# Low halves of the second weight forms made by a negative copy on ScalarE and an adding DMA from GpSimd

## The chip, the cores and the metric

One core of one Trainium2 chip runs the whole program. The metric is the device time of one execution in microseconds. The core has TensorE (PE: matrix products, results in PSUM banks), VectorE (DVE), ScalarE (ACT), GpSimd (POOL), SyncE (SP, which here only issues loads) and 16 DMA engines.

## The reference, cut to what matters

Two layers on 512 tokens of width 1024, all in fp32. Each layer has two feed-forward blocks (FFNs) around an attention and a mixing part:

```python
def swiglu(x, wgu, wd):
    gate, up = jnp.split(x @ wgu, 2, axis=-1)
    return (jax.nn.silu(gate) * up) @ wd
...
h = h + 0.5 * swiglu(rms_norm(h, ffn1_norm[i]), ffn1_wgu[i], ffn1_wd[i])
```

The hidden width is 2816, that is 22 tiles of 128. The change touches only the four FFNs (F = 0 to 3).

## The kernel before, in words

Every fp32 operand is split into a rounded high half (ACT copies it into a tensor of type fp32r) and a low half, operand minus high half. A product is three matmuls: high by high, high by low, low by high.

In an FFN the first 4 hidden tiles are computed plainly. The other 18 (`FAST = 18`, numbered q) are "half-size products": the weights of a tile are four blocks a21, a22, a11, a12, loaded into `sraw[q % 2]` by two DMAs of 512 KB from SP. A fast matrix scheme with fewer block products, each on 256 token columns instead of 512, needs sums of these blocks. For each q there are

- `form_sums(q)` (DVE, three instructions, L1427, L1431, L1433): block sums into `sums`, of which there is only one copy. Its first instruction waits for `second_forms` of q-1;
- the first forms, `form_hi`/`form_lo`, 2048 wide: `first_plain` and `first_sums`, each a copy on ACT (L798, L804) and a subtraction on DVE (L1437, L1442);
- the second forms, `more_hi`/`more_lo`, two buffers of 1536: `second_plain(q)` (512 wide, from `sraw`; ACT L812, then DVE L1447) and `second_sums(q)` (1024 wide, from `sums`; ACT L816, then DVE L1452). The DVE halves of these two are what is replaced. The first raises `s_split`, which lets SP load tile q+2 into the same `sraw` buffer; the second raises `second_forms`, which lets PE start step 4 of q and DVE overwrite `sums`.

PE's order is written out by hand. In iteration n it does step 1 of tile n, step 4 of tile n-1, some down-projection products (`gap(n, 0)`), steps 2 and 3 of tile n, `gap(n, 1)`, steps 5 and 6 of tile n-1, and `gap(n, 2)`. A gap of the iterations from n = 4 on has 3, 3 and 2 such products; in iterations 1 to 3 it has 2, 1 and 1. Step 2 of q needs `first_sums(q)`; step 4 of q needs `second_forms` of q.

The orders on the other engines are fixed too. In iteration n >= 4 DVE does: product of tile n-2, `second_plain(n)`, low half of the hidden tile n-2, sums into h, `second_sums(n)`, `gate0(n)`, `first_plain(n+1)`, `up1(n-1)`, sums into h, `form_sums(n+1)`, perhaps a `down_split`, `first_sums(n+1)`, sums into h, perhaps a `down_split`, `gate1(n-1)` (L1401), and the rest of tile n-1. With r = (n-4) mod 3, two of the `down_split`s lie before `gate1` at r = 0, one at r = 2 and none at r = 1. In iterations 1 to 3 `gate1(n-1)` comes before `first_sums(n+1)`. ACT ends its iteration n with

```python
if n:
    fast_silu_(n - 1)
if n and n + 1 < FAST:
    second_plain(n + 1)
    second_sums(n + 1)
```

and `fast_silu_(n-1)` (L782) waits for `gate1(n-1)` (`x_read`). ACT's next work is `fast_hid(n-1)` (L787) and `copy_y(n+1)` (L825). GpSimd has no work inside the loop before: its first waiting instruction is the clearing of `sumsq` after the last `second_forms` of the FFN.

Of the kernel before, what the change touches and what calls it, by code (L numbers as in the profile page):

```python
# [108 lines left out]
def macaron_kernel(nc, x, mem, positions, ffn1_norm, ffn1_wgu, ffn1_wd, mix_norm, w_in,  # L109
# [12 lines left out]
    with ctx:  # L122
        def sem(name):
            return ctx.enter_context(nc.semaphore(name))
# [213 lines left out]
        wn_ready = sem("wn_ready")  # L338
        d_done = sem("d_done")
# [96 lines left out]
        def fast_no(F, q):  # L436
            return F * FAST + q + 1
# [51 lines left out]
        def _(sp):  # L489
# [25 lines left out]
            def ffn_loads(L, up, wgu, wd):  # L515
                F = 2 * L + (up == UP2)
                for kind, i in FFN_ORDER:
                    if kind == "S":
                        if i < 2:
                            sp.wait_ge(w_used, used(L, up + 1))  # L520
                        else:
                            sp.wait_ge(s_split, fast_no(F, i - 2))
                        col = fast_tile(i) * P
                        for a, c in ((1024, col), (0, col + FF)):
                            sp.dma_start(sraw[i % 2][:, a:a + 1024].rearrange("p (k c) -> p k c", c=P),
                                         wgu[L, :, c:c + P].rearrange("(k p) c -> p k c", p=P)).then_inc(s_loaded[i % 2], 16)
                        continue
# [49 lines left out]
        def _(pool):  # L577
# [36 lines left out]

            for L in range(0, LAYERS):
                inverse_rms(L * 4 + 1)
                stage_sums(L, 0, 1)
# [22 lines left out]
                inverse_rms(L * 4 + 4)  # L640
                stage_sums(L, 3, 4)
# [4 lines left out]
        def _(act):  # L646
# [99 lines left out]
            def ffn(L, f, up, stage, rb_no, gain, next_gain, next_unit):  # L746
# [60 lines left out]
                def second_plain(q):  # L807
                    if q < 2:
                        act.wait_ge(n_done, F + 1)
                    else:  # L810
                        act.wait_ge(second_product, step_no(F, q - 2, 3))
                    act.activation(more_hi[:, q % 2, 1024:1536], sraw[q % 2][:, 512:1024], ACT.Copy).then_inc(second_rounded, 1)  # L812

                def second_sums(q):
                    act.wait_ge(form_summed, 3 * fast_no(F, q))
                    act.activation(more_hi[:, q % 2, 0:1024], sums[:, 0:2, :].rearrange("p a c -> p (a c)"), ACT.Copy)\  # L816
                       .then_inc(second_rounded, 1)
# [379 lines left out]
        def _(dve):  # L1197
# [124 lines left out]
            def ffn(L, f, up, stage, stat_no, next_gain, next_unit):  # L1322
# [122 lines left out]
                def second_plain(q):  # L1445
                    dve.wait_ge(second_rounded, 2 * (fast_no(F, q) - 1) + 1)
                    dve.tensor_tensor(out=more_lo[:, q % 2, 1024:1536], in0=sraw[q % 2][:, 512:1024],  # L1447
                                      in1=more_hi[:, q % 2, 1024:1536].bitcast(f32), op=ALU.subtract).then_inc(s_split, 1)

                def second_sums(q):  # L1450
                    dve.wait_ge(second_rounded, 2 * fast_no(F, q))
                    dve.tensor_tensor(out=more_lo[:, q % 2, 0:1024], in0=sums[:, 0:2, :].rearrange("p a c -> p (a c)"),  # L1452
                                      in1=more_hi[:, q % 2, 0:1024].bitcast(f32), op=ALU.subtract).then_inc(second_forms, 1)

# [43 lines left out]
                if at_first:  # L1498
# [32 lines left out]
                    second_plain(0)  # L1531
# [4 lines left out]
                    second_sums(0)  # L1536
# [6 lines left out]
                else:  # L1543
# [28 lines left out]
                    second_plain(0)  # L1572
# [4 lines left out]
                    second_sums(0)  # L1577
# [10 lines left out]
                for n in range(FAST):  # L1588
# [3 lines left out]
                    if n >= 2:  # L1592
                        fast_product_(n - 2)
                        second_plain(n)
# [6 lines left out]
                    if n >= 4:  # L1601
                        second_sums(n)
                    gate0(n)
                    gate0_scale(n)
                    if n in (2, 3):
                        second_sums(n)
# [4 lines left out]
                    if n == 0:  # L1611
                        second_plain(1)
                        second_sums(1)
# [1054 lines left out]
```

## Time and profile before

| | |
|---|---|
| Time before | 2100.7 us, median of 2 runs (2100.58 to 2100.82) |
| Span of the profiled execution | 2098.5 us; its own time is not listed apart, and the runs lie 2.1 to 2.3 us above the span |
| PE | 2084.8 us busy, 99% of the span |
| VectorE | 1645.2 us, 78% |
| ScalarE | 986.8 us, 47% |
| GpSimd | 149.6 us, 7% |
| DMA | 212.14 MB, mean 101 GB/s |
| TensorE clock granted | 0.998 of full |

PE is the engine to watch: it is busy all through the span. The busy share of another engine says how full its queue is, not whether it delays anything.

### The profile page before, as it was taken

The page shows a single profiled execution, that of the slowest core. Times are in us where ns is not written, and L with a number is a line of the kernel's source. Part 1 is how long each engine was busy: PE and PEld are TensorE (multiplying, and loading weights), DVE is VectorE, ACT ScalarE, POOL GpSimd, SP SyncE. Part 2 cuts the span into 40 slices and gives each one's busy share as a digit, 9 for nine tenths or more (in the row PEclk, how much of TensorE's full clock was granted, in tenths as well). Part 3 has the DMA queues.
Part 4 walks back from the last instruction along what each step waited for, and adds up shares of the span by engine and source line. Part 5 has one row for each costly group of instructions (what it writes and reads, how often), then busy time and mean ns, then how long its engine had stood idle before and what let it go on. Part 6 is the DMA issues. An engine that isn't in the chain of part 4 may idle for free.

```text
span 2098.5 us, 32639 instructions
## 1 busy us (share of the span) xinstructions
PE 2084.8 (99%) x13143; PEld 1867.3 (89%) x13143; DVE 1645.2 (78%) x2460; ACT 986.8 (47%) x1491; POOL 149.6 (7%) x114
## 2 busy tenths in 40 slices
PE   9999999999999999999999999999999999999998
PEld 7999998889888889999889999988898888999997
DVE  7998886658654789888799988766686458898885
ACT  6444444446433544444454444343464345444442
POOL 0000003100120300000110000030002111000001
PEclk9999999999999999999999999999999999999999
DMA  6333323323231343332233333243233224333321
GB/s 197 101 112 99 103 86 113 124 81 101 96 106 41 92 129 107 118 100 91 75 116 116 106 111 106 66 142 99 81 102 104 77 66 135 91 111 103 100 85 56
DMA packets 268018, 212.14 MB, mean 101 GB/s; under 512 B 7422, under 2 KB 234332, under 8 KB 267868
## 3 DMA queue, kind: packets, MB, share of 16 engines
q1 hardware_dynamic: 264608, 205.55, 31.5%
q10 hardware_dynamic: 3260, 4.51, 0.8%
q8 instruction: 105, 1.72, 0.3%
q14 instruction: 45, 0.37, 0.1%
HBM read 207.93 MB, written 2.10 MB: 100 GB/s over the span
## 4 chain that ended last, share of the span: by engine, by line
PE 98%; ACT 1%; issue 0%; DVE 0%; POOL 0%; POOLq 0%; DVEq 0%; ACTq 0%
PE ps L2004 21%; PE ps L2005 20%; PE ps L2006 20%; PE ps L2220 11%; PE ps L2222 11%; PE ps L2221 11%; PE ps L2493 1%; PE ps L2451 0%; PE ps L2371 0%; PE ps L2561 0%; PE ps L2298 0%; PE ps L2498 0%; PE ps L2025 0%; PE ps L2018 0%; PE ps L2047 0%
## 5 line engine op out<-in xcount | busy, mean ns | idle before, releaser
L2005 PE MATMUL ps<-hid_lo,wn_hi 128*128 128x512 f32 x640 | 251.7, 393 | 0.0
L2004 PE MATMUL ps<-hid_hi,wn_hi 128*128 128x512 f32 x640 | 251.5, 393 | 0.0
L2006 PE MATMUL ps<-hid_hi,wn_lo 128*128 128x512 f32 x640 | 249.0, 389 | 0.0
L1473 DVE SCALAR_TENSOR_TENSOR h<-ps,h 128x512 f32<-128x512 f32 x224 | 153.0, 685 | 31.3 <-PE ps L2006 31.0
L668 ACT ACTIVATE w_hi<-raw 128x2048 fp32r<-128x2048 f32 x61 | 116.8, 1915 | 123.6 <-PE ps L2006 91.4
L2220 PE MATMUL ps<-t_hi,form_hi 128*128 128x256 f32 x576 | 159.6, 277 | 0.0
L2222 PE MATMUL ps<-t_hi,form_lo 128*128 128x256 f32 x576 | 159.6, 277 | 0.0
L2220 PE MATMUL ps<-hn_hi,form_hi 128*128 128x256 f32 x576 | 159.5, 277 | 0.0
L2222 PE MATMUL ps<-hn_hi,form_lo 128*128 128x256 f32 x576 | 159.4, 277 | 0.0
L2222 PE MATMUL ps<-t_hi,more_lo 128*128 128x256 f32 x576 | 159.3, 277 | 0.0
L2221 PE MATMUL ps<-t_lo,form_hi 128*128 128x256 f32 x576 | 159.2, 276 | 0.0
L2221 PE MATMUL ps<-hn_lo,form_hi 128*128 128x256 f32 x576 | 159.2, 276 | 0.0
L2220 PE MATMUL ps<-t_hi,more_hi 128*128 128x256 f32 x576 | 159.0, 276 | 0.0
L2221 PE MATMUL ps<-t_lo,more_hi 128*128 128x256 f32 x576 | 159.0, 276 | 0.0
L1203 DVE TENSOR_TENSOR w_lo<-raw,w_hi 128x2048 fp32r<-128x2048 f32 x49 | 114.3, 2333 | 48.8 <-ACT w_hi L668 48.7
L2004 PE MATMUL ps<-hn_hi,w_hi 128*128 128x512 f32 x376 | 147.8, 393 | 0.6 <-DVE w_lo L1275 0.5
L2006 PE MATMUL ps<-hn_hi,w_lo 128*128 128x512 f32 x376 | 146.6, 390 | 0.0
L2005 PE MATMUL ps<-hn_lo,w_hi 128*128 128x512 f32 x376 | 146.4, 389 | 0.0
L2006 PEld LDWEIGHTS ps<-hid_hi,wn_lo 128*128 128x128 f32 x640 | 120.3, 188 | 26.8
L597 POOL TENSOR_TENSOR sumsq<-sumsq,tmp 128x512 f32<-128x512 f32 x63 | 111.1, 1764 | 371.7 <-ACT tmp L679 366.1
L2004 PEld LDWEIGHTS ps<-hid_hi,wn_hi 128*128 128x128 f32 x640 | 120.1, 188 | 19.3
L2005 PEld LDWEIGHTS ps<-hid_lo,wn_hi 128*128 128x128 f32 x640 | 120.1, 188 | 16.4
(344 smaller groups left out, 5975.6 us busy)
## 6 DMA issues: line engine op xcount, KB each, us to landing
sraw<-in_ffn_wgu_dram SPq DMA_DIRECT2D x144, 512.0 KB, 4.9
raw<-in_ffn_wd_dram SPq DMA_DIRECT2D x48, 512.0 KB, 3.8
raw<-in_ffn_wd_dram SPq DMA_DIRECT2D x80, 256.0 KB, 4.1
raw<-in_w_in_dram SPq DMA_DIRECT2D x40, 512.0 KB, 4.4
raw<-in_cross_wkv_dram SPq DMA_DIRECT2D x32, 512.0 KB, 4.0
raw<-in_ffn_wgu_dram SPq DMA_DIRECT2D x30, 512.0 KB, 4.8
raw<-in_w_out_dram SPq DMA_DIRECT2D x16, 512.0 KB, 4.3
raw<-in_cross_wq_dram SPq DMA_DIRECT2D x16, 512.0 KB, 3.8
```

Of the source, the lines that this page charges most:

```text
L597: pool.tensor_tensor(out=sumsq[:, :], in0=sumsq[:, :], in1=tmp[:, m2, :], op=ALU.add)\
L668: act.activation(w_hi[:, s, :], raw[:, s, :], ACT.Copy).then_inc(w_rounded, 1)
L1203: dve.tensor_tensor(out=w_lo[:, s, 0:z], in0=raw[:, s, 0:z], in1=w_hi[:, s, 0:z].bitcast(f32), op=ALU.subtract).then_inc(w_split, 1)
L1473: dve.scalar_tensor_tensor(out=h[:, m, :], in0=ps[:, down_bank(c, m), :], scalar=0.5, in1=h[:, m, :], op0=ALU.mult, op1=ALU.add).then_inc( ...
L2004: pe.matmul(dst, a_hi, b_hi, start=start, stop=False)
L2005: pe.matmul(dst, a_hi, b_lo, start=False, stop=False)
L2006: return pe.matmul(dst, a_lo, b_hi, start=False, stop=stop)
L2220: pe.matmul(dst, a_hi, b_hi, start=start and k == 0, stop=False, skip_group_check=not start)
L2221: pe.matmul(dst, a_hi, b_lo, start=False, stop=False, skip_group_check=not start)
L2222: last = pe.matmul(dst, a_lo, b_hi, start=False, stop=k == 3, skip_group_check=not start)
L2493: pe.matmul(ps[:, 4 + 2 * b + br, 0:N], q_part[r, hd, q], k_part[r, hd, 0:N], start=n == 0, stop=False)
```

## The change

The low half is made by another route. Instead of `raw - hi` on DVE, ACT writes `-raw` (rounded to fp32r, scale -1.0) into `more_lo` right behind the copy into `more_hi`, and a DMA issued from GpSimd adds `raw` to it in place. Each tile q then has two such DMAs, of 256 KB (128 x 512 fp32) and 512 KB (128 x 1024). GpSimd waits for the first to land before it raises `s_split` and before it issues the second, and waits for the second before it raises `second_forms`. SP's wait before the load of tile q+2 also names `first_forms` of q. DVE's two subtractions go.

```diff
--- before.py
+++ after.py
@@ -336,6 +336,7 @@
         n_done = sem("n_done")
         wn_rounded = sem("wn_rounded")
         wn_ready = sem("wn_ready")
+        low_added = sem("low_added")
         d_done = sem("d_done")
         d_read = sem("d_read")
         hid_rounded = sem("hid_rounded")
@@ -520,6 +521,7 @@
                             sp.wait_ge(w_used, used(L, up + 1))
                         else:
                             sp.wait_ge(s_split, fast_no(F, i - 2))
+                            sp.wait_ge(first_forms, 2 * fast_no(F, i - 2))
                         col = fast_tile(i) * P
                         for a, c in ((1024, col), (0, col + FF)):
                             sp.dma_start(sraw[i % 2][:, a:a + 1024].rearrange("p (k c) -> p k c", c=P),
@@ -612,8 +614,22 @@
                     if (L, stage, m) != (LAYERS - 1, 3, KT - 1):
                         add_square(tile_no(L, stage, m) - KT, sum_no(L, stage, m) - 1, m % 2)
 
+            def second_lows(F):
+                for q in range(FAST):
+                    b = q % 2
+                    pool.wait_ge(second_rounded, 2 * (fast_no(F, q) - 1) + 1)
+                    pool.dma_start(more_lo[:, b, 1024:1536], sraw[b][:, 512:1024], accum_op=ALU.add).then_inc(low_added, 16)
+                    pool.wait_ge(low_added, 16 * (2 * fast_no(F, q) - 1))
+                    pool.sem_inc(s_split, 1)
+                    pool.wait_ge(second_rounded, 2 * fast_no(F, q))
+                    pool.dma_start(more_lo[:, b, 0:1024], sums[:, 0:2, :].rearrange("p a c -> p (a c)"), accum_op=ALU.add)\
+                        .then_inc(low_added, 16)
+                    pool.wait_ge(low_added, 16 * 2 * fast_no(F, q))
+                    pool.sem_inc(second_forms, 1)
+
             for L in range(0, LAYERS):
                 inverse_rms(L * 4 + 1)
+                second_lows(2 * L)
                 stage_sums(L, 0, 1)
                 inverse_rms(L * 4 + 2)
                 pool.wait_ge(small_loaded, L * 64 + 64)
@@ -638,6 +654,7 @@
                 inverse_rms(L * 4 + 3)
                 stage_sums(L, 2, 3)
                 inverse_rms(L * 4 + 4)
+                second_lows(2 * L + 1)
                 stage_sums(L, 3, 4)
             inverse_rms(LAYERS * 4 + 1)
 
@@ -809,12 +826,15 @@
                         act.wait_ge(n_done, F + 1)
                     else:
                         act.wait_ge(second_product, step_no(F, q - 2, 3))
-                    act.activation(more_hi[:, q % 2, 1024:1536], sraw[q % 2][:, 512:1024], ACT.Copy).then_inc(second_rounded, 1)
+                    act.activation(more_hi[:, q % 2, 1024:1536], sraw[q % 2][:, 512:1024], ACT.Copy)
+                    act.activation(more_lo[:, q % 2, 1024:1536], sraw[q % 2][:, 512:1024], ACT.Copy, scale=-1.0)\
+                       .then_inc(second_rounded, 1)
 
                 def second_sums(q):
                     act.wait_ge(form_summed, 3 * fast_no(F, q))
-                    act.activation(more_hi[:, q % 2, 0:1024], sums[:, 0:2, :].rearrange("p a c -> p (a c)"), ACT.Copy)\
-                       .then_inc(second_rounded, 1)
+                    act.activation(more_hi[:, q % 2, 0:1024], sums[:, 0:2, :].rearrange("p a c -> p (a c)"), ACT.Copy)
+                    act.activation(more_lo[:, q % 2, 0:1024], sums[:, 0:2, :].rearrange("p a c -> p (a c)"), ACT.Copy,
+                                   scale=-1.0).then_inc(second_rounded, 1)
 
                 def copy_y(q):
                     act.wait_ge(first_product, step_no(F, q, 1))
@@ -1442,16 +1462,6 @@
                     dve.tensor_tensor(out=form_lo[:, 1024:2048], in0=sums[:, 2:4, :].rearrange("p a c -> p (a c)"),
                                       in1=form_hi[:, 1024:2048].bitcast(f32), op=ALU.subtract).then_inc(first_forms, 1)
 
-                def second_plain(q):
-                    dve.wait_ge(second_rounded, 2 * (fast_no(F, q) - 1) + 1)
-                    dve.tensor_tensor(out=more_lo[:, q % 2, 1024:1536], in0=sraw[q % 2][:, 512:1024],
-                                      in1=more_hi[:, q % 2, 1024:1536].bitcast(f32), op=ALU.subtract).then_inc(s_split, 1)
-
-                def second_sums(q):
-                    dve.wait_ge(second_rounded, 2 * fast_no(F, q))
-                    dve.tensor_tensor(out=more_lo[:, q % 2, 0:1024], in0=sums[:, 0:2, :].rearrange("p a c -> p (a c)"),
-                                      in1=more_hi[:, q % 2, 0:1024].bitcast(f32), op=ALU.subtract).then_inc(second_forms, 1)
-
                 def third_split(half):
                     u = up + FFN_AT["N", 3]
                     dve.wait_ge(wn_rounded, wn_rounded_no(F, 1 + half))
@@ -1528,12 +1538,10 @@
                     add_part(0, 1)
                     whole_gate(3)
                     add_part(0, 2)
-                    second_plain(0)
                     add_part(0, 3)
                     whole_scale(3)
                     whole_product(3)
                     add_part(0, 4)
-                    second_sums(0)
                     add_part(0, 5)
                     whole_low(3)
                     add_part(0, 6)
@@ -1569,12 +1577,10 @@
                     first_plain(0)
                     first_sums(0)
                     whole_gate(3)
-                    second_plain(0)
                     whole_scale(3)
                     add_part(0, 0)
                     whole_product(3)
                     add_part(0, 1)
-                    second_sums(0)
                     add_part(0, 2)
                     whole_low(3)
                     add_part(0, 3)
@@ -1591,26 +1597,19 @@
                         form_sums(1)
                     if n >= 2:
                         fast_product_(n - 2)
-                        second_plain(n)
                     if n == 4:
                         down_split(c, 0)
                     if n >= 2:
                         hid_low(fast_tile(n - 2), G[:, n % 2, :])
                     if n:
                         add_gap(n - 1, 2)
-                    if n >= 4:
-                        second_sums(n)
                     gate0(n)
                     gate0_scale(n)
-                    if n in (2, 3):
-                        second_sums(n)
                     if n == 0 and at_first:
                         form_sums(1)
                     if n + 1 < FAST:
                         first_plain(n + 1)
                     if n == 0:
-                        second_plain(1)
-                        second_sums(1)
                         first_sums(1)
                         add_gap(0, 1)
                         down_split(1, 2)
```

## Rows read from the trace of the kernel before

**Rows 1.** The page: busy time, share of the span and instructions of each engine.

```profile
PE 2084.8 (99%) x13143; PEld 1867.3 (89%) x13143; DVE 1645.2 (78%) x2460; ACT 986.8 (47%) x1491; POOL 149.6 (7%) x114
```

**Rows 2.** The chain of work that ended last, shares of the span.

```profile
PE 98%; ACT 1%; issue 0%; DVE 0%; POOL 0%; POOLq 0%; DVEq 0%; ACTq 0%
```

**Rows 3.** Busy time by window: length, PE, PEld, DVE, ACT, POOL, clock, DMA share, GB/s.

```profile
205.72:220.82 15.10, 15.10 (x110) 14.10 (x109) 13.98 (x21) 7.41 (x12) 0.00 (x0) 1.00 0.40 123
```

**Rows 4.** Starts of copy_y (L825) on ACT: start, duration, iterations 1, 4, 5, 11.

```profile
81.08 0.38 ACT L825 ACTIVATE G<-ps 128x256 f32<-128x256 f32 x1 [1.53 <-PE ps L2222]
...
118.66 0.39 ACT L825 ACTIVATE G<-ps 128x256 f32<-128x256 f32 x1 [1.18 <-DVE hid_lo L1374]
...
133.16 0.38 ACT L825 ACTIVATE G<-ps 128x256 f32<-128x256 f32 x1 [0.82 <-PE ps L2222]
...
223.76 0.38 ACT L825 ACTIVATE G<-ps 128x256 f32<-128x256 f32 x1 [1.71 <-PE ps L2222]
```

**Rows 5.** Groups by form: the two DVE subtractions that are taken out.

```profile
L1452 DVE TENSOR_TENSOR more_lo<-sums,more_hi 128x1024 fp32r<-128x1024 f32 x72 | 87.6, 1217 | 0.0
...
L1447 DVE TENSOR_TENSOR more_lo<-sraw,more_hi 128x512 fp32r<-128x512 f32 x72 | 49.3, 684 | 0.0
```

**Rows 6.** Timeline of DVE, iterations 10 (r = 0) and 11 (r = 1).

```profile
208.19 1.22 DVE L1452 TENSOR_TENSOR more_lo<-sums,more_hi 128x1024 fp32r<-128x1024 f32 x1
...
212.69 1.21 DVE L1427 TENSOR_TENSOR sums<-sraw 128x1024 f32<-128x1024 f32 x1
...
216.14 1.22 DVE L1442 TENSOR_TENSOR form_lo<-sums,form_hi 128x1024 fp32r<-128x1024 f32 x1
...
218.74 0.42 DVE L1401 TENSOR_TENSOR G<-ps,rb 128x256 f32<-128x256 f32 x1
...
227.20 1.21 DVE L1427 TENSOR_TENSOR sums<-sraw 128x1024 f32<-128x1024 f32 x1
...
231.02 1.23 DVE L1442 TENSOR_TENSOR form_lo<-sums,form_hi 128x1024 fp32r<-128x1024 f32 x1 [1.16 <-ACT form_hi L804]
...
233.37 0.42 DVE L1401 TENSOR_TENSOR G<-ps,rb 128x256 f32<-128x256 f32 x1 [0.52 <-PE ps L2222]
```

**Rows 7.** Timeline of ACT at the end of iteration 10.

```profile
219.19 0.63 ACT L782 ACTIVATE G<-G 128x512 f32<-128x512 f32 x1 [1.40 <-DVE G L1401]
219.73 0.61 ACT L812 ACTIVATE more_hi<-sraw 128x512 fp32r<-128x512 f32 x1
220.25 1.05 ACT L816 ACTIVATE more_hi<-sums 128x1024 fp32r<-128x1024 f32 x1
221.41 0.63 ACT L787 ACTIVATE hid_hi<-G 128x512 fp32r<-128x512 f32 x1
```

**Rows 8.** The first iterations: ACT's second_plain(1); DVE of iteration 1; PE's step 2 of tile 2.

```profile
74.05 0.63 ACT L812 ACTIVATE more_hi<-sraw 128x512 fp32r<-128x512 f32 x1
...
84.79 1.22 DVE L1427 TENSOR_TENSOR sums<-sraw 128x1024 f32<-128x1024 f32 x1
...
89.05 0.42 DVE L1401 TENSOR_TENSOR G<-ps,rb 128x256 f32<-128x256 f32 x1
89.38 1.22 DVE L1442 TENSOR_TENSOR form_lo<-sums,form_hi 128x1024 fp32r<-128x1024 f32 x1
...
95.95 0.28 PE L2220 MATMUL ps<-t_hi,form_hi 128*128 128x256 f32 x1
```

**Rows 9.** DMA issues: count, KB each, median us from issue to landing; the fourth are the output stores.

```profile
sraw<-in_ffn_wgu_dram SPq DMA_DIRECT2D x144, 512.0 KB, 4.9
...
raw<-in_ffn_wd_dram SPq DMA_DIRECT2D x80, 256.0 KB, 4.1
...
raw<-in_cross_wq_dram SPq DMA_DIRECT2D x16, 512.0 KB, 3.8
...
out_dram<-o_sb SPq DMA_DIRECT2D x8, 256.0 KB, 2.6
```

**Rows 10.** The tile sraw: landing of its 144 loads.

```profile
DMA to landing us min/median/max: 3.6/4.9/8.0
```

## The prediction

> **What bounds the kernel now.** I read the page's busy shares first: PE is busy 2084.8 of 2098.5 us and VectorE 78% [rows 1]. Then the chain of work that ended last, where the reader should see that 98% of the span lies on PE and nothing on VectorE [rows 2]. So at most 13.7 us could be won by any help to another engine, 0.7%, and the question is only whether the change makes PE wait. Then I read one iteration of the inner loop over the 18 half-size tiles. PE fills 15.10 of 15.10 us, VectorE 13.98 [rows 3]. The starts of copy_y show the period: from iteration 1 to iteration 4 37.58 us, 12.5 each; from 5 to 11 90.60, 15.10 each; between them iteration 4 with 14.5, whose copy_y started late, behind VectorE [rows 4]. VectorE is nearly full, yet never late for PE.
>
> **What is removed.** 72 subtractions of 1217 ns and 72 of 684 ns, 136.9 us of VectorE, 1.9 us per iteration [rows 5]. None of it is on PE's path, so its worth is nothing as long as PE is the bound; what it buys is slack.
>
> **What ACT gets.** Per tile a second copy of each width. The copies start 0.52 us and, for the wide one, about 1 us apart (219.73 to 220.25, and 1.05 long) [rows 7]: 1.5 us, 108 us in all, of an engine that is 47% busy. Directly behind them in ACT's queue stand fast_hid and copy_y. fast_hid moves from 221.41 to about 222.9, ends at 223.5 and copy_y, due at 223.76 [rows 4, 7], isn't moved. I cost it at nothing; were that cover gone, it would be up to 1.5 us per iteration.
>
> **SP and GpSimd.** SP's load of tile q+2 now waits for the first adding DMA, some 4 us more, and lands some 5 us after its issue [rows 9]. ACT's first copy of that tile comes an iteration later, so this is hidden by about 8 us. The extra wait for first_forms of q is met an iteration earlier. GpSimd has no other work in the loop, and what follows there waited for the last second_forms before too.
>
> **The wait that decides.** There is one copy of sums, so form_sums(q+1) on VectorE waits for second_forms(q), and VectorE works in order: queued behind that wait are first_sums(q+1), additions into h, the down_splits and gate1(q-1). For gate1 ACT's silu waits, and behind the silu stands second_plain(q+1), which starts the two DMAs of the next tile. This is a ring. Call T(q) the time of second_forms(q), and D the time from the end of ACT's narrow negative copy to second_forms: two DMAs one after the other, with their semaphore hops. The steps of one turn:
> - form_sums to the end of gate1. At r = 0: 212.69 to 219.16, 6.5 us. At r = 1: 227.20 to 233.79, 6.6, of which 1.3 is waiting for PE that falls away when PE is behind, so 5.3. At r = 2 one down_split less than at r = 0 leaves 5.7. Mean 5.8 [rows 6].
> - silu to the next ACT start, 219.19 to 219.73: 0.55. Then the narrow copies, 0.52 and 0.63: 1.15 [rows 7]. With a hop, 1.75.
> - D.
>
> So a turn takes 7.6 + D in the later iterations. In iterations 1 to 3 gate1 comes earlier (84.79 to 89.47 is 4.7 us in iteration 1 [rows 8]; without waits 4.3 is my mean of the three) and a turn takes 6.1 + D. Before, this ring was never tight: more_lo was ready at 209.4, 3.3 us before form_sums wanted it [rows 6]. Now a turn costs PE nothing only if 7.6 + D is under 15.1 and 6.1 + D under 12.5. The wide copy pair (2.1 us) is over before the first DMA lands, so it isn't in the ring.
>
> **Slack at the start.** With the second copy ACT's second_plain(1) ends at 75.2 [rows 8]; with D near 9.6 T(1) is 84.8, when form_sums(2) began before, so nothing is lost yet. first_sums(2) is then ready at 90.6 and PE wants it at 95.95 [rows 8]: 5.3 us. In later iterations form_sums to first_sums takes 4.7 us (212.69 to 217.36 [rows 6]) against 5.8 here, and one more down product lies ahead of step 2: some 7 us in all.
>
> **The sum.** 16 turns lead from T(1) to T(17): three of the early kind and 13 of the later, one of these against 14.5. The loss of one FFN is 3 (D + 6.1 - 12.5) + 13 (D + 7.6) - (12 x 15.1 + 14.5) - 7 = 16 D - 123 us, or nothing if negative. The point from which it counts is D = 7.7 us. Each us of D beyond that costs 64 us over the four FFNs.
>
> **What D is.** No row shows an adding DMA, or one from GpSimd. Nearest below: 2.6 us for a 256 KB store and 3.8 for a 512 KB load [rows 9], with 0.3 for each hop 7.0: no loss. Nearest in the loop: 4.1 for a 256 KB load and 4.9 for the 512 KB loads of sraw [rows 9], with 0.6 for hops 9.6. I take this one, because the second DMA runs beside the 1 MB load of sraw that its own s_split has just let go, as those loads run beside each other. If the add moves twice the bytes, and from 256 to 512 KB a landing grows by 0.8 [rows 9], the two take 4.9 and 6.5, and D is 12.0. At the upper end the second takes the longest landing of sraw, 8.0 [rows 10], and the first 4.9: 13.5. Below zero nothing is possible here: a DMA can't land before it is issued. With D = 9.6 the loss is 30.6 us per FFN, 122 in all; on 2100.7 (span 2098.5 and the 2.2 around it) that is 2223.
>
> The Trainium skill (DMA: Bandwidth & Descriptors, section Anatomy of one DMA) gives a GpSimd-issued DMA 2.0 us plus its bytes over 436 GB/s. An estimate by that page is 2.6 and 3.2 us, D under 7, and by it the change would cost nothing; no run here shows such a DMA yet.
>
> The Trainium skill (Collectives: The Full Stack, section The bandwidth ceiling) says that an add in a DMA needs two source reads and so gets half the rate. By that page the two would be 3.2 and 4.4 us, an estimate that ends at the edge of the ring's room; the rows show no add.
>
> **Rivals.**
> 1. *Hidden (not slower).* The two DMAs with hops take under 8.4 us: 16 x 8.4 - 123 is 11.4 per FFN, 46 in all, 2.2%; and up to 7.7 nothing, 2100 to 2142. For it: stores of SBUF data land in 2.6 us [rows 9], both ends here are SBUF, and the ring's room is real. Against it: two DMAs strictly one after the other, each through GpSimd, and the second beside a 1 MB load. Likeliest in it is no change, 2101. The first page sentence above is this case. Chance 0.24.
> 2. *A costly add.* D of 11 or more, from reading the destination too: 2312 at 11, 2377 at 12.0, 2473 at 13.5. For it: two reads and a write per element, and an instruction that GpSimd must expand. Against it: the DMA engines are 40% busy in the iteration shown [rows 3], so bytes alone aren't scarce. Chance 0.31.
> 3. *The relief of VectorE pays.* Only if PE waited on it; 13.7 us of idle PE bound it. Over 2% chance 0.01; under 2% it is inside rival 1.
> 4. *It doesn't do what it says*, for instance an add that is split in many small transfers: then D is far above 13.5 and the time over 2473. It is in the tail of rival 2.
>
> **How the numbers follow.** My forecast, D from 8.4 to 11, 2143 to 2312, has 0.44; rival 1 0.24; rival 2 0.31; faster 0.01. The time is that of D = 9.6, 2223. Under 2100 and over 2473 I leave 0.13 together. 2% (42 us) is about what a measurement of this kernel tells from no change; hence slower 0.75, same 0.24, faster 0.01.
>
> **What would show it.** In the profile after: VectorE's form_sums preceded by idle time put down to second_forms or a DMA, 2 to 5 us each, and PE idle before steps 2 and 4 (form_hi or more_hi of L2220), once per iteration from iteration 3 or 4 on; the period of copy_y near 7.6 + D (17.2) instead of 15.10; early ones near 15.7. VectorE busy 137 us less and ACT 108 more. The two DMAs of a tile landing 4 to 5 us after issue. The forecast is wrong in the sum if the period is right and the slack is not; in D if the landings are shorter or longer; in its mechanism if the period stretches while form_sums doesn't wait, as it would if ACT's later fast_hid were what PE waits for. A period still of 15.10 with form_sums waiting says rival 1.

## The result and the profile after

The changed kernel takes 2465.45 us, the median of 2 runs, against 2100.7: the ratio is 1.1736, 95% interval 1.1702 to 1.177. That is 365 us more, where 122 were forecast. The range, up to 2473, just holds it.

The page of the changed kernel: busy time and instructions by engine; by queue, the packets, MB and share of 16 DMA engines; the chain that ended last; and the DMA issues (count, KB each, median us from issue to landing).

```profile
PE 2205.1 (89%) x13143; PEld 1957.1 (79%) x13143; DVE 1525.3 (62%) x2316; ACT 1073.4 (44%) x1635; POOL 273.8 (11%) x258
...
q0 software_dynamic: 20736, 56.63, 12.0%
...
PE 46%; DMA 31%; DVE 11%; issue 6%; ACT 5%; POOLq 0%; DVEq 0%; SPq 0%; POOL 0%; ACTq 0%
DMA more_lo<-sums 21%; PE ps L2003 13%; PE ps L2005 13%; PE ps L2004 13%; DMA more_lo<-sraw 10%; DVE sums L1447 3%; DVE sums L1451 2%; ACT more_hi L829 2%; ACT more_lo L830 1%; PE ps L2219 1%; DVE h L1483 1%; DVE wn_lo L1475 1%; PE ps L2221 1%; PE ps L2220 1%; DVE form_lo L1462 1%
...
sraw<-in_ffn_wgu_dram SPq DMA_DIRECT2D x144, 512.0 KB, 6.0
more_lo<-sums POOLq DMA_DIRECT2D x72, 512.0 KB, 8.5
...
more_lo<-sraw POOLq DMA_DIRECT2D x72, 256.0 KB, 3.2
```

The chain that was 98% PE [rows 2] now has 31% of DMA, VectorE and ScalarE between: the two adding DMAs are links of it. The narrow one lands in 3.2 us, the wide one in 8.5. VectorE lost 119.9 us of work and ScalarE gained 86.6 (neighbouring instructions overlap, so both are less than the sums of durations that the prediction gave, 137 and 108).

One turn of the ring, from the chain of the changed kernel, in order of time (start, us, what):

```profile
256.70 1.24 DVE sums L1447
...
261.98 0.34 DVE G L1421
262.34 0.03 ACT G L799
...
263.50 0.53 ACT more_lo L830
264.03 0.28 issue
264.31 3.20 DMA more_lo<-sraw
...
268.07 8.54 DMA more_lo<-sums
276.61 0.02 issue
276.63 0.03 POOLq L628
...
276.75 1.24 DVE sums L1447
```

It is the ring of the prediction link by link: form_sums, gate1 (5.6 us later, as the 5.7 reckoned for r = 2), silu, narrow copies, narrow DMA, wide DMA, and form_sums of the next tile, 20.05 us after the last. Only the last DMA is long. The waits say the same (who, whom, us, times, longest), first VectorE and then PE:

```profile
DVE sums L1447 <- POOLq L628: 392.6, 64, 9.3
...
PE ps L2003 <- DVE h L1483: 80.6, 20, 6.0
PE ps L2219 <- DVE U L1416: 56.0, 11, 7.2
PE ps L2003 <- DVE hid_lo L1394: 53.2, 16, 3.5
PE ps L2003 <- DVE wn_lo L1475: 50.1, 18, 4.1
```

VectorE waits 64 times for `second_forms`, and PE then for whatever VectorE does late. The engine for which PE waits is not the cause; one has to go one step further back. The loop window of the first FFN (length, PE, PEld, DVE, ACT, POOL busy, clock, DMA share, GB/s):

```profile
72.30:410.00 337.70, 276.82 (x1766) 254.30 (x1766) 190.17 (x278) 135.78 (x205) 27.98 (x33) 0.89 0.47 114
```

These 337.7 us took 241.6 before, when PE was full throughout [rows 3 shows one iteration]. The granted clock is down to 0.89.

The wide DMA of the last tile of an FFN is the hint on which the experiments rest. No load of `sraw` follows it. GpSimd's timeline there:

```profile
407.07 0.84 POOL L621 DMA_DIRECT2D more_lo<-sraw  x1 [12.21 <-ACT more_lo L830]
411.33 0.85 POOL L625 DMA_DIRECT2D more_lo<-sums  x1 [3.41 <-DMA more_lo<-sraw]
415.92 0.53 POOL L594 MEMSET sumsq<- 128x512 f32 x1 [3.73 <-POOLq L628]
```

From its start to the next work it takes 4.6 us, not 8.7.

The mean DMA share of 0.47 over the loop hides what happens while the wide DMA runs. For the one that starts at 268.07 us, the window (columns as above) and the two queues of DMAs, q1 with the loads from SP and q0 with GpSimd's DMAs (packets, MB, share of the 16 engines' time in that window):

```profile
268.07:276.61 8.54, 8.54 (x47) 7.94 (x47) 2.60 (x5) 1.89 (x4) 0.85 (x1) 0.74 0.77 184
...
q1 hardware_dynamic: 2080, 1.05, 46.1%
q0 software_dynamic: 144, 0.52, 30.9%
```

The 16 engines are 77% busy there, and 96% from 269 to 275 us. The load's packets take 3.9 of the 8.5 us, the wide DMA's own 2.6.

### The profile page after: what moved, and what is told of

It reads as the page before. It is cut to its first block, busy times and chain, and to the rows that moved or that the text cites. A ratio compares the mean times of both kernels' runs of the same rounds, so it can differ in the third digit from the quotient of the medians.

```text
span 2464.9 us, 32991 instructions
## 1 busy us (share of the span) xinstructions
PE 2205.1 (89%) x13143; PEld 1957.1 (79%) x13143; DVE 1525.3 (62%) x2316; ACT 1073.4 (44%) x1635; POOL 273.8 (11%) x258
## 4 chain that ended last, share of the span: by engine, by line
PE 46%; DMA 31%; DVE 11%; issue 6%; ACT 5%; POOLq 0%; DVEq 0%; SPq 0%; POOL 0%; ACTq 0%
DMA more_lo<-sums 21%; PE ps L2003 13%; PE ps L2005 13%; PE ps L2004 13%; DMA more_lo<-sraw 10%; DVE sums L1447 3%; DVE sums L1451 2%; ACT more_hi L829 2%; ACT more_lo L830 1%; PE ps L2219 1%; DVE h L1483 1%; DVE wn_lo L1475 1%; PE ps L2221 1%; PE ps L2220 1%; DVE form_lo L1462 1%
## 5 line engine op out<-in xcount | busy, mean ns | idle before, releaser
L2003 PE MATMUL ps<-hid_hi,wn_hi 128*128 128x512 f32 x640 | 269.9, 422 | 183.9 <-DVE h L1483 80.6
L1447 DVE TENSOR_TENSOR sums<-sraw 128x1024 f32<-128x1024 f32 x72 | 88.2, 1225 | 392.6 <-POOLq L628 392.6
L2003 PEld LDWEIGHTS ps<-hid_hi,wn_hi 128*128 128x128 f32 x640 | 125.1, 196 | 220.3 <-DVE h L1483 88.6
L821 ACT ACTIVATE form_hi<-sums 128x1024 fp32r<-128x1024 f32 x72 | 76.3, 1060 | 444.0 <-DVE sums L1451 444.0
L2004 PE MATMUL ps<-hid_lo,wn_hi 128*128 128x512 f32 x640 | 263.6, 412 | 0.0
L2005 PE MATMUL ps<-hid_hi,wn_lo 128*128 128x512 f32 x640 | 261.9, 409 | 0.0
L621 POOL DMA_DIRECT2D more_lo<-sraw x72 | 62.0, 861 | 1154.6 <-ACT more_lo L830 1121.9
L2219 PE MATMUL ps<-hn_hi,form_hi 128*128 128x256 f32 x576 | 177.7, 309 | 0.0
L2220 PE MATMUL ps<-hn_lo,form_hi 128*128 128x256 f32 x576 | 176.2, 306 | 0.0
L2221 PE MATMUL ps<-hn_hi,form_lo 128*128 128x256 f32 x576 | 174.7, 303 | 0.0
L2219 PEld LDWEIGHTS ps<-t_hi,more_hi 128*128 128x128 f32 x576 | 112.7, 196 | 58.3 <-issue 58.1
L2003 PE MATMUL ps<-hn_hi,w_hi 128*128 128x512 f32 x376 | 147.8, 393 | 0.7 <-DVE w_lo L1295 0.5
```

The costliest lines, as they stand in the source:

```text
L621: pool.dma_start(more_lo[:, b, 1024:1536], sraw[b][:, 512:1024], accum_op=ALU.add).then_inc(low_added, 16)
L821: act.activation(form_hi[:, 1024:2048], sums[:, 2:4, :].rearrange("p a c -> p (a c)"), ACT.Copy)\
L1447: dve.tensor_tensor(out=sums[:, 1:3, :], in0=sraw[q % 2][:, 512:1536].rearrange("p (a c) -> p a c", c=512), in1=a21.unsqueeze(1).to_broadc ...
L2003: pe.matmul(dst, a_hi, b_hi, start=start, stop=False)
L2004: pe.matmul(dst, a_hi, b_lo, start=False, stop=False)
L2005: return pe.matmul(dst, a_lo, b_hi, start=False, stop=stop)
```

## The experiments

The table sums up what the experiments below measured in the ring. The terms are means over the four FFNs, from the timelines: from the start of form_sums to the start of the first adding DMA (tiles 5 to 16); from there to the start of the wide one (tiles 2 to 16); from there to the next form_sums (tiles 1 to 15); and the whole turn from form_sums to form_sums (tiles 4 to 15). As the tiles differ, a turn is the sum of its terms only within 0.3 us. "By the sum" puts D = 0.3 + the two DMA columns into the prediction's own 16 D - 123 us per FFN, on 2100.7.

| kernel | form_sums to DMA | narrow to wide | wide to form_sums | turn | by the sum | measured |
|---|---|---|---|---|---|---|
| the change | 7.83 | 4.36 | 8.70 | 21.1 | 2464 | 2465 |
| head_start | 7.83 | 4.07 | 7.46 | 19.5 | 2366 | 2370 |
| no_add | 7.80 | 3.62 | 6.59 | 18.1 | 2281 | 2287 |
| sums_only | 9.19 | - | 8.62 | 18.0 | 2267 | 2268 |
| late_load | 7.83 | 4.02 | 4.88 | 16.7 | 2198 | 2215 |
| together | 7.82 | 1.92 | 5.89 | 15.5 | 2128 | 2134 |
| together_late | 8.13 | 1.92 | 5.08 | 14.9 | 2101 | 2109 |

(For sums_only the 1.36 us by which its first column is longer go into D. The room of the ring in the later iterations, 15.1 less 7.8, is 7.3 us for the two DMAs.)

**late_load.** The load of sraw is let go only after the wide DMA.

```diff
                     pool.wait_ge(low_added, 16 * (2 * fast_no(F, q) - 1))
-                    pool.sem_inc(s_split, 1)
                     ...
                     pool.wait_ge(low_added, 16 * 2 * fast_no(F, q))
                     pool.sem_inc(second_forms, 1)
+                    pool.sem_inc(s_split, 1)
```

> s_split, which lets the next 1 MB load of sraw start, is raised only when the second adding DMA has landed. Theory (the second DMA is slow because that load runs beside it): its time falls from 8.7 us to about the 4.6 us that the last tile of each FFN shows, where no load follows; D falls from 13.2 to about 9.2, and with the ring's sum of 16 D - 123 us per FFN, plus 14 us for the early turns, the kernel takes 2200 to 2245 us. Rival (an adding DMA of 512 KB takes that long by itself): the second DMA stays near 8.7 us and the time near 2465.

2214.84 us, ratio 1.0543 (1.0508 to 1.0577). The page of this kernel:

```profile
more_lo<-sums POOLq DMA_DIRECT2D x72, 512.0 KB, 4.5
...
more_lo<-sraw POOLq DMA_DIRECT2D x72, 256.0 KB, 3.2
```

The wide DMA falls from 8.5 to 4.5 us, and with it go 250 of the 365 us. The rival is out: it isn't the size of the transfer. It was the 1 MB load that the change itself starts, by its own s_split, half a us ahead of the wide DMA. The queues during one wide DMA of this kernel, 280.78 to 285.22 us:

```profile
q0 software_dynamic: 144, 0.52, 60.8%
```

Its own packets take 2.7 us of the 16 engines' time, as in the change; the load's 3.9 us are gone, and the landing is 4.0 us shorter.

**together.** Both DMAs issued without a wait for the first landing, with a semaphore each.

```diff
+                    no = fast_no(F, q)
-                    pool.wait_ge(low_added, 16 * (2 * fast_no(F, q) - 1))
-                    pool.sem_inc(s_split, 1)
                     pool.wait_ge(second_rounded, 2 * fast_no(F, q))
-                    pool.dma_start(... sums ...).then_inc(low_added, 16)
-                    pool.wait_ge(low_added, 16 * 2 * fast_no(F, q))
+                    pool.dma_start(... sums ...).then_inc(sums_added, 16)
+                    pool.wait_ge(low_added, 16 * no)
+                    pool.sem_inc(s_split, 1)
+                    pool.wait_ge(sums_added, 16 * no)
                     pool.sem_inc(second_forms, 1)
```

> Both adding DMAs are issued without a wait for the first one's landing in between, each with a semaphore of its own; s_split is raised when the first has landed. Theory (the ring adds D to each turn, and D is the sum of the two landings): the second DMA now starts about 2 us after the first instead of 4.4, so D is about 2.2 + 8.7 = 10.9, or less where the load starts later than it, and the kernel takes 2290 to 2345 us. Rival (the 16 DMA engines' bytes are what is scarce, whatever the order): the landings lengthen by what the overlap saves, and the time stays above 2420.

2134.04 us, ratio 1.0158 (1.0129 to 1.0188): below both ranges. I had kept 8.7 us for the wide DMA. It took 5.7, as it was now issued ahead of the load (the next kernel tests this). GpSimd's timeline in this kernel, then SP's:

```profile
213.43 0.84 POOL L623 DMA_DIRECT2D more_lo<-sraw  x1 [13.98 <-ACT more_lo L832]
215.32 0.85 POOL L625 DMA_DIRECT2D more_lo<-sums  x1 [1.05 <-ACT more_lo L838]
```

```profile
216.69 1.93 SPq L528 DMA_DIRECT2D sraw<-in_ffn_wgu_dram  x2
```

**head_start.** The change with one line moved, to issue the wide DMA ahead of the load:

```diff
-                    pool.sem_inc(s_split, 1)
                     pool.wait_ge(second_rounded, 2 * fast_no(F, q))
                     pool.dma_start(... sums ...).then_inc(low_added, 16)
+                    pool.sem_inc(s_split, 1)
                     pool.wait_ge(low_added, 16 * 2 * fast_no(F, q))
```

> As the change, but s_split is raised right after the second adding DMA is issued, not right before. The load of sraw then comes about 1 us behind the DMA's issue instead of about even with it. Theory (who is queued first matters: in the kernel with both DMAs issued together the second had 1.3 us of head start and landed in 5.7 us beside the same load): the second DMA lands in 5.7 to 6.8 us, D is about 10.1 to 11.2, the kernel takes 2265 to 2345 us. Rival (only the overlap in bytes counts): it still takes about 8.5 us and the time is above 2430.

2369.65 us, ratio 1.1282 (1.126 to 1.1305), between the theory's range and the rival's. The head start was not 1 us. GpSimd's timeline here, then SP's:

```profile
253.40 0.86 POOL L624 DMA_DIRECT2D more_lo<-sums  x1 [2.64 <-DMA more_lo<-sraw]
```

```profile
253.42 0.99 SPq L527 DMA_DIRECT2D sraw<-in_ffn_wgu_dram  x2
```

The two are issued together, and the wide DMA lands in 7.1 us (median). The four kernels give a row: load issued 0.5 us before the wide DMA, 8.5 us; 0.02 after, 7.1; 1.4 after, 5.7; not beside it, 4.5. The first 0.5 us of lead are worth 1.4 us, the next 1.4 us another 1.4. What the lead changes is how much of the load's work is done before the wide DMA lands: by the queues, as read above (medians of 24 tiles), the load's packets take 3.8, 3.1, 0.6 and 0 us of the 16 engines' time in it. The 4.5 us alone and that time added give 8.3, 7.6, 5.1 and 4.5, within 0.6 us of the landings. (In together the last of the narrow DMA runs there too.) Of the 96 us between the change and this kernel some 19 aren't the load's: with the semaphore raised later, the wide DMA is also issued 0.3 us sooner after the narrow one (4.07 against 4.36).

**together_late.** Both edits; the diff is against together.

```diff
                     pool.wait_ge(low_added, 16 * no)
-                    pool.sem_inc(s_split, 1)
                     pool.wait_ge(sums_added, 16 * no)
                     pool.sem_inc(second_forms, 1)
+                    pool.sem_inc(s_split, 1)
```

> Both edits: the two adding DMAs without a wait in between, and the load of sraw let go only after both have landed. Theory: D is about 2.2 + 5 = 7 to 8 us, at the ring's room of 7.7, so the kernel takes 2100 to 2150 us. Rival (bytes scarce, or an add that is slow by itself): above 2300.

2108.99 us, ratio 1.004 (1.0024 to 1.0056), with the same adds, bytes and instructions as the change. The DMAs now just fit the ring's room: VectorE still waits 32 times for second_forms, 27 us in all, but PE waits for VectorE some 5 us in the whole kernel. What is left is act_only's, below.

**no_add.** Plain copies from GpSimd in place of the adds; it leaves the addition out, so more_lo is not the low half.

```diff
-                    pool.dma_start(..., accum_op=ALU.add)
+                    pool.dma_start(...)
```

> The changed kernel with both DMAs as plain copies: it leaves out the addition, so more_lo holds the whole operand and not its low half. It tells what the add costs. Theory A (the add costs little, the load beside it and the fixed part cost most): the two DMAs still take about 3.2 and 8 us to land and the time is above 2400 us. Theory B (the add reads twice and doubles the moving part): they take about 2.6 and 5 us, D about 8.5 to 10, and the time is 2170 to 2270 us.

2286.9 us, ratio 1.0886 (1.0854 to 1.0917), between the two theories. The page of this kernel:

```profile
more_lo<-sums POOLq DMA_DIRECT2D x72, 512.0 KB, 6.4
...
more_lo<-sraw POOLq DMA_DIRECT2D x72, 256.0 KB, 2.2
```

The add costs 1.0 us on the narrow DMA and 2.1 on the wide one beside the load. With no load beside it, in the last tile of an FFN, GpSimd's timeline has 3.0 us from the wide copy to the next work, against 4.6 with the add: 1.6 us, of which 0.3 is GpSimd's longer issue (0.85 against 0.53).

```profile
2232.98 0.53 POOL L625 DMA_DIRECT2D more_lo<-sums  x1 [2.40 <-DMA more_lo<-sraw]
2236.02 0.53 POOL L594 MEMSET sumsq<- 128x512 f32 x1 [2.52 <-POOLq L628]
```

So theory A was wrong to give the add almost nothing, and B to give it half.

**sums_only and plain_only.** One of the two low halves by DMA, the other still subtracted on VectorE as before.

```diff
 # sums_only: second_plain as before, and on GpSimd only
+                    pool.wait_ge(second_rounded, 2 * no)
+                    pool.dma_start(more_lo[..., 0:1024], sums ..., accum_op=ALU.add).then_inc(low_added, 16)
+                    pool.wait_ge(low_added, 16 * no)
+                    pool.sem_inc(second_forms, 1)
 # plain_only: second_sums as before, and on GpSimd only
+                    pool.wait_ge(second_rounded, 2 * (no - 1) + 1)
+                    pool.dma_start(more_lo[..., 1024:1536], sraw[b] ..., accum_op=ALU.add).then_inc(low_added, 16)
+                    pool.wait_ge(low_added, 16 * no)
+                    pool.sem_inc(s_split, 1)
```

> Only the wide low half (second_sums) goes by the negative copy and the adding DMA; the narrow one stays a subtraction on VectorE, which also raises s_split. Theory (ring): the wide DMA starts about 1.8 us after where the narrow one started, and there is no first landing to wait for; beside the load, which is now issued a little before it, it takes 7 to 8.7 us, so D counts as 8.8 to 10.5 and the kernel takes 2185 to 2300 us. Rival (the cost lies in having GpSimd and the DMA in the path at all, about the same for each of the two): half of the change's 365 us or more, above 2283, with the DMA near 5 us.

2268.19 us, ratio 1.0799 (1.0772 to 1.0827). It is inside the theory's range, and the wide DMA took 8.3 us to land, not the 5 of the rival; the load is again issued ahead of it, by 0.4 us in the median (at 252.42 against 253.05 in one turn of the timeline).

> Only the narrow low half (second_plain) goes by the negative copy and the adding DMA; the wide one stays a subtraction on VectorE and raises second_forms. Theory (ring): this DMA is then outside the ring, since form_sums waits only for second_forms; its landing is wanted by PE's step 6 more than an iteration later. Time within 0.5% of before, 2095 to 2112 us. Rival (the narrow DMA carries its share of the cost, 4.4 of the 13.2 us): 2170 to 2250 us.

2100.97 us, ratio 1.0003 (0.9993 to 1.0012). The narrow DMA still lands in 3.2 us; nobody in the ring waits for it. It costs nothing and VectorE is 43 us less busy, which gains nothing either, as PE is the bound. The wide DMA is gone from this kernel, so it speaks for the narrow one alone.

**ring_open.** The change with the orders of VectorE and ScalarE altered from iteration 4 on, so that gate1 and the silu don't stand behind form_sums.

```diff
 # VectorE
                         up1(n - 1)
                         add_gap(n, 0)
-                        if n + 1 < FAST:
-                            form_sums(n + 1)
                         ...
                         fast_scale(n - 1)
+                        if n + 1 < FAST:
+                            form_sums(n + 1)
+                            first_sums(n + 1)
 # ScalarE
-                    if n + 1 < FAST:
+                    if n < 4 and n + 1 < FAST:
                         first_sums(n + 1)
                     ...
                         second_plain(n + 1)
+                        if n >= 4:
+                            first_sums(n + 1)
                         second_sums(n + 1)
```

> The change with the orders of VectorE and ScalarE altered from iteration 4 on: form_sums(n+1) and first_sums(n+1) come after fast_scale(n-1) on VectorE, and ScalarE's first_sums(n+1) after second_plain(n+1). gate1, the silu and the narrow copies no longer stand behind the wait for second_forms, though both DMAs take as long as in the change. Theory: a late turn is then form_sums and the wide copies (5.1 us), a hop and the second DMA (8.7), 14.1 us, under PE's 15.1; only the three early turns of each FFN still lose, up to 17 us each FFN. 2110 to 2175 us. Rival (the DMAs' own time is what is lost, wherever the waits stand): above 2300.

2243.3 us, ratio 1.0681 (1.0659 to 1.0702): neither. A turn is 16.2 us in most of the later iterations, and no longer because of the DMA: by the waits of this kernel, VectorE waits for second_forms only 12 times (in the early iterations), but 36 times for PE before gate1 (L1423):

```profile
DVE h L1485 <- PE ps L2006: 75.2, 66, 2.5
DVE sums L1449 <- POOLq L628: 70.4, 12, 8.7
DVE G L1423 <- PE ps L2222: 63.1, 36, 2.1
```

The new order closed another ring. The copies of the wide form and of first_sums stand in ScalarE's queue before fast_hid; its timeline in this kernel:

```profile
253.47 1.07 ACT L821 ACTIVATE form_hi<-sums 128x1024 fp32r<-128x1024 f32 x1 [1.78 <-DVE sums L1453]
254.45 1.05 ACT L835 ACTIVATE more_hi<-sums 128x1024 fp32r<-128x1024 f32 x1
255.39 1.05 ACT L836 ACTIVATE more_lo<-sums 128x1024 fp32r<-128x1024 f32 x1
256.44 0.63 ACT L804 ACTIVATE hid_hi<-G 128x512 fp32r<-128x512 f32 x1
```

fast_hid and copy_y come late, PE waits 20 times for gate0 (17.5 us), and form_sums now stands behind gate1, which waits for PE's step 6. This is read from the orders and the waits; no run tests it alone. So opening the ring is worth 222 us with the wide DMA nearly as slow as before (7.8 us). Of the 143 us that are left, some 59 lie in the later turns (16.3 us on the mean over 15.1) and the rest in the early ones; what the right order would give was not found.

**act_only.** The kernel before with ScalarE's negative copies, and VectorE's subtractions over them.

```diff
-                    act.activation(more_hi[...], sraw[...], ACT.Copy).then_inc(second_rounded, 1)
+                    act.activation(more_hi[...], sraw[...], ACT.Copy)
+                    act.activation(more_lo[...], sraw[...], ACT.Copy, scale=-1.0).then_inc(second_rounded, 1)
 # and the same for the wide copy from sums
```

> The kernel before with ScalarE's two negative copies added and nothing else: VectorE's subtractions follow and overwrite them, no DMA from GpSimd. It measures what I costed at nothing. Theory: 2098 to 2108 us, no difference beyond 0.3%. Rival (1.5 us more on ScalarE per iteration delays fast_hid and through it VectorE, which is 93% full here): 2120 to 2200 us.

2107.99 us, ratio 1.0036 (1.0024 to 1.0047): 7.5 us, just outside the 0.3% and inside the range in us. copy_y of iterations 2, 3 and 4 in this kernel (93.75, 105.73, and 118.66 [rows 4] before):

```profile
94.39 0.38 ACT L828 ACTIVATE G<-ps 128x256 f32<-128x256 f32 x1 [0.82 <-DVE hid_lo L1377]
107.11 0.38 ACT L828 ACTIVATE G<-ps 128x256 f32<-128x256 f32 x1 [0.82 <-DVE hid_lo L1377]
120.91 0.39 ACT L828 ACTIVATE G<-ps 128x256 f32<-128x256 f32 x1 [1.17 <-DVE hid_lo L1377]
```

The early iterations have no room for a later fast_hid: the starts are 0.6, 1.4 and 2.3 us late, and from iteration 9 on they stay 2.2 late. So 2 us per FFN are lost there. In together_late the same three starts are 0.9, 1.7 and 2.7 us late, so most of its 8.5 us is this too.

**filler.** The change, with PE kept running where it waits.

```diff
+                    if 2 <= n < FAST:
+                        pe.wait_ge(x_read, fast_no(F, n - 2))
+                        pe.wait_ge(u0_read, fast_no(F, n - 2))
+                        keep_busy(14, pair(n + 1))
                     gap(n, 0)
                     ...
                     gap(n, 1)
+                    if 2 <= n < FAST:
+                        keep_busy(14, pair(n + 1))
                     if n:
                         fast_step(n - 1, 5, 6)
```

> The change, with two times 14 idle transposes on PE per iteration from iteration 2 on, put where PE waits (ahead of gap(n, 0) and ahead of step 5), into a bank that nothing uses then. They keep PE from standing still, so the granted clock, 0.89 to 0.91 in the loops of the change, should rise. Theory (the late turns' ring holds no PE work, and only the early turns pass through PE's step 6 at half clock): the clock rises and the time stays within 1.5% of the change, 2430 to 2475 us. Rival (PE's halved clock is a main part of the stretched turns): with the clock back at 0.97 or more the time falls below 2400.

2473.26 us, ratio 1.1774 (1.1751 to 1.1798). The first loop's window:

```profile
72.30:410.00 337.70, 309.77 (x2222) 287.68 (x2221) 191.71 (x282) 136.01 (x207) 28.84 (x34) 0.96 0.47 115
```

The granted clock rises from 0.89 to 0.96 in this window and from 0.943 to 0.979 in the whole kernel, and the time doesn't fall. The added work has a cost of its own, so this doesn't price the clock exactly; but the 16 turns from the second tile to the last got only 3 us shorter per FFN (323 against 326 us), 12 us in all. The halved clock is a result of the waits and not a main cause of the loss.

## Why the prediction was right in kind and wrong in size

The mechanism was the forecast one, shown from both sides: in plain_only the one DMA left is outside the ring and costs nothing, together_late makes both DMAs fit and costs 0.4%, and the table's turns are the sums of their terms within 0.3 us. By the prediction's steps:

- *The bound, and what is removed.* Right. plain_only frees VectorE and gains nothing.
- *form_sums to the first DMA, 7.6 plus a hop of 0.3.* Measured 7.83.
- *The sum, 16 D - 123.* With the table's terms it gives 2464 for 2465, and 1 to 17 us too little for the other kernels. Part of this is luck. The 16 turns that the sum counts end with the DMAs of the last tile, which the table's means leave out and beside which no load runs. With it (means over tiles 2 to 17) D is 12.9 us in the change and the sum gives 2434, 31 us low; in the others it is 8 to 33 us low. Two reasons are in the traces. The early turns weren't 6.1 + D: ScalarE's second_plain waits there for PE's step 6 behind up1, not for gate1, and form_sums to the DMA (tiles 2 to 4) took 7.3 us in the change and 7.0 in late_load, against 6.1 and a hop of 0.3. That is 11 us in the change. And the slack of 7 us per FFN was too large: the measured turns, put in place of the reckoned ones, leave 2.0 us of it in the change, another 20 us in all.
- *D.* This is the step that failed: "Nearest in the loop: 4.1 for a 256 KB load and 4.9 for the 512 KB loads of sraw [rows 9], with 0.6 for hops 9.6." The first term measured 4.36 instead of 4.4, by two errors that cancel: the landing was 3.7 us on the mean (3.2 in the median; 23 of 72 took over 3.6), the hop to the next DMA 0.56. The second measured 8.70 with its hops instead of 5.2. D was 13.4 instead of 9.6 by the table, and 3.76 us at 64 us each are 241 of the 242 that were missing; with the last tile counted, 3.3 us and some 211, the others being those of the step above.
- *Why it failed.* The prediction saw the load ("the second DMA runs beside the 1 MB load of sraw that its own s_split has just let go") and took for it the landing of the loads, as if a DMA beside that load fared as they do. The transfer was costed as a size. Alone it is 4.6; the load adds up to 4, and how far ahead of the load the DMA is issued decides how much of that (head_start, together). The prediction also argued that "the DMA engines are 40% busy in the iteration shown [rows 3], so bytes alone aren't scarce". That share is a mean over the iteration: while the wide DMA and the load run together the engines are 96% busy (269 to 275 us of the change), and what lengthens the one is the engines' time that the other takes. The range held by its upper end, 4.9 + 8.0 + 0.6 = 13.5, whose second term was the longest landing of a load and not a DMA beside one.
- *The add moves twice the bytes.* That estimate gave 4.9 and 6.5 us for the two, and the add did cost: 1.0 us on the narrow one, and 1.6 alone and 2.1 beside the load on the wide one. But most of the wide one's 8.5 us is not the add.
- *ScalarE at nothing.* Off by 7.5 us. I had checked copy_y against fast_hid's end, but copy_y waits for hid_low on VectorE, which comes after it, and I had looked at a late iteration, where the period leaves room, not at the early ones, where it doesn't.
- *SP's wait hidden by 8 us.* Right: no engine waits for a landing of sraw, in late_load neither, where the load starts some 5 us later still.
- *What would show it.* The idle before form_sums was 6.1 us on the mean (392.6 over 64 times), not 2 to 5, and the period 21, not 17.2. PE's idle time was not where it was looked for: 184 us of it lie before down products (L2003), which wait for VectorE's sums into h, hid_low and down_splits, 56 us before a second-form product that waits for up1, and 5.5 us before a first-form one.

Of rival 1, the point from which it decides was right: the two DMAs of together_late stay under the room. Rival 2 named a D over 11 and this is where the case ended, but for a reason of which it held only half: without the add the change is 179 us faster, without the load beside it 250. The two sum to more than 365. The add costs 0.5 us more beside the load than alone, and with both gone D would be 6.4 us by the table's differences, an estimate that no run tests: under the 7.7 from which a DMA costs anything, so the last 1.3 us of it would win nothing.

The Trainium skill (DMA: Bandwidth & Descriptors, section Anatomy of one DMA) gives 2.0 us plus the bytes over 436 GB/s, an estimate of 2.6 and 3.2 us for the two without an add. no_add shows plain copies from GpSimd with 2.2, and 2.8 to 2.9 for the wide one with no load beside it. The trace is some 0.4 us under it. The Trainium skill (Collectives: The Full Stack, section The bandwidth ceiling) says of the exchange between cores that an add needs two source reads and so gets half the rate; carried over to this DMA that is an estimate of 3.2 and 4.4 us. 3.2 and 4.4 (the shortest landing) were measured. The totals agree and the parts only roughly: the halved rate would add 0.6 and 1.2 us to the plain copy, and the add cost 1.0 and 1.6. Both hold for a DMA alone; neither section gives the 8.5 beside a load.

## What to carry to other kernels

A latency put into a ring (one buffer, an in-order engine, a wait that ends where it began) costs its whole excess over the ring's room, once per turn: find the ring, measure its room, and price the new link in the company it will have. Look at what the change itself releases just ahead of the new link; here moving one semaphore increment was worth 250 of 365 us, and not waiting between two independent DMAs another 106 on top. Read the DMA share in the stretch where the link runs, not over the loop. An engine at 78% busy behind a full PE is no reason to move its work.

## What the runs showed of the hardware

- A 512 KB adding DMA from GpSimd within SBUF took 4.5 us to land alone and 8.5 beside a 1 MB load from SP issued 0.5 us before it. The 16 DMA engines were 47% busy over the loop, and 96% from 269 to 275 us, where both ran. The load's two DMAs took 6.0 us each against 4.9 [rows 9], so both pay.
- The landing was, within 0.6 us, the landing alone plus the time that the load's packets took on the 16 engines in it: 4.5 + 3.8 for 8.5 in the change, 4.5 + 3.1 for 7.1 in head_start, 4.5 + 0.6 for 5.7 in together, and 2.9 + 3.9 for 6.4 in no_add.
- The add in a GpSimd DMA cost 1.0 us over a plain copy at 256 KB (3.2 against 2.2), 1.6 us at 512 KB alone and 2.1 us at 512 KB beside the load. The packets of the wide DMA took 2.7 us of the 16 engines' time with the add and 1.4 without.
- The granted clock fell to 0.50 (the 1.2 GHz level) in stretches that followed PE's waits, such as 268 to 272 us of the change after PE had been busy 0.8 of 4 us, and was back at full in 274 to 277 us.
- GpSimd was busy 0.85 us with each issue of an adding DMA, 0.53 us with each of a plain one, and its next DMA started after the landing for which it waited by 0.56 us in the change, where it raises a semaphore in between, and by 0.28 us in late_load, where it doesn't.
